# Norm weights applied to the tokens before they are turned, and another order of work in the turn between stages

## What is computed

```python
def rms_norm(x, g):
    y = x * lax.rsqrt(jnp.mean(x * x, axis=-1, keepdims=True) + EPS)
    return y * g

y = stage(rms_norm(x, pre_g[l]))          # ffn, hybrid, memory, ffn / sparse, relu
x = x + scale * rms_norm(y, post_g[l])    # scale 0.5 or 1
```

## Time and profile before

| | |
|---|---|
| runs, us | 1981.7, 1980.12, 1981.13; median 1981.13 |
| profiled execution, us | 1982.36, span 1980.6 |
| PE busy | 1877.0 us (95%) |
| DVE, ACT, POOL busy | 1309.5, 1084.0, 199.5 us |
| mean granted TensorE clock | 0.988 of full |
| DMA | 333 MB, mean 168 GB/s |

### The profile page before, as it was taken

How to read it: one execution, slowest core, us unless ns; L and a number is a source line. 1 busy time by engine, 2 the same in 40 slices (tenths; PEclk the granted TensorE clock), 3 DMA queues, 4 the chain that set the end, 5 groups by cost and what they waited for, 6 DMA issues and landing times.

```text
span 1980.6 us, 28155 instructions
## 1 busy us (share of the span) xinstructions
PE 1877.0 (95%) x10911; PEld 1627.6 (82%) x10911; DVE 1309.5 (66%) x1830; ACT 1084.0 (55%) x1647; POOL 199.5 (10%) x252
## 2 busy tenths in 40 slices
PE   6999998999999999999999899999988999988998
PEld 5888897878888888889887778888867888877887
DVE  5776756665766676666675667666866666766665
ACT  5655544555655565554465566556655445755443
POOL 1010101010000011001020000002100110300111
PEclk9999998999999999999999999999999999999999
DMA  8586643234465557657423527555434564533552
GB/s 264 194 283 191 174 156 105 94 137 153 151 221 191 171 175 238 233 138 221 139 67 122 174 87 223 191 188 168 149 128 158 186 199 155 202 107 128 193 190 85
DMA packets 228389, 333.23 MB, mean 168 GB/s; under 512 B 22230, under 2 KB 178016, under 8 KB 228256
## 3 DMA queue, kind: packets, MB, share of 16 engines
q1 hardware_dynamic: 222112, 307.96, 47.9%
q0 software_dynamic: 6144, 23.49, 3.5%
HBM read 330.38 MB, written 1.05 MB: 167 GB/s over the span
## 4 chain that ended last, share of the span: by engine, by line
PE 85%; DVE 7%; ACT 6%; issue 1%; DMA 1%; POOL 0%; DVEq 0%; SPq 0%; ACTq 0%
PE ps L1635 82%; PE ps L1640 3%; ACT region L691 2%; ACT ahl L691 2%; DVE ahl L1102 2%; DVE xn L1094 1%; DVE wlo L1094 1%; ACT whi L691 1%; DVE xs L1102 1%; DVE region L1094 1%; DMA raw<-ffn_w_gate 1%; DVE mlo L1094 0%; DVE sm L1110 0%; DVE region L1102 0%; ACT mhi L691 0%
## 5 line engine op out<-in xcount | busy, mean ns | idle before, releaser
L1094 DVE TENSOR_TENSOR wlo<-raw,whi 128x1024 fp32r<-128x1024 f32 (+2 forms) x458 | 559.7, 1222 | 199.2 <-ACT whi L691 162.1
L691 ACT ACTIVATE whi<-raw 128x1024 fp32r<-128x1024 f32 (+2 forms) x458 | 483.0, 1055 | 61.6 <-PE ps L1635 15.1
L1635 PE MATMUL ps<-ahl,whi 128*128 128x512 f32 (+1 forms) x1936 | 434.7, 351 | 2.5 <-DVE region L1094 2.1
L1635 PEld LDWEIGHTS ps<-ahl,whi 128*128 128x128 f32 x1936 | 333.4, 190 | 44.9 <-DVE region L1094 2.3
L1635 PE MATMUL ps<-whi,ahl 128*128 128x512 f32 (+2 forms) x1160 | 319.5, 352 | 32.8 <-DVE ahl L1102 28.5
L691 ACT ACTIVATE region<-ps 128x512 f32<-128x512 f32 (+2 forms) x260 | 150.1, 577 | 338.2 <-PE ps L1635 282.4
L1635 PE MATMUL ps<-ahl,wlo 128*128 128x256 f32 x1568 | 271.4, 282 | 0.0
L1635 PEld LDWEIGHTS ps<-whi,ahl 128*128 128x128 f32 x1160 | 207.4, 192 | 68.6 <-DVE ahl L1102 37.9
L1635 PEld LDWEIGHTS ps<-ahl,wlo 128*128 128x128 f32 x1568 | 234.2, 191 | 11.7
L1635 PE MATMUL ps<-wlo,ahl 128*128 128x512 f32 (+2 forms) x580 | 199.2, 343 | 0.0
L1094 DVE TENSOR_TENSOR mlo<-raw,mhi 128x1024 fp32r<-128x1024 f32 x130 | 159.0, 1223 | 54.9 <-ACT mhi L691 44.7
(11 more groups left out here) (164 smaller groups left out, 2417.3 us busy)
## 6 DMA issues: line engine op xcount, KB each, us to landing
raw<-w_ff SPq DMA_DIRECT2D x64, 1024.0 KB, 5.3
raw<-ffn_w_gate SPq DMA_DIRECT2D x44, 1024.0 KB, 5.4
raw<-ffn_w_up SPq DMA_DIRECT2D x44, 1024.0 KB, 5.6
raw<-ffn_w_down SPq DMA_DIRECT2D x44, 1024.0 KB, 4.9
raw<-w_in SPq DMA_DIRECT2D x38, 1024.0 KB, 5.4
raw<-w_out SPq DMA_DIRECT2D x16, 1024.0 KB, 4.9
raw<-xa_wk SPq DMA_DIRECT2D x8, 1024.0 KB, 5.2
raw<-xa_wv SPq DMA_DIRECT2D x8, 1024.0 KB, 5.1
```

The source lines that it names most:

```text
L691: e.activation(o, i, f, **kw).then_inc(*act.did(*names))
L1094: e.tensor_tensor(o, a, b, op).then_inc(*dve.did(*names))
L1635: m = e.matmul(o, l, r, start=start, stop=stop)
```

## The change

The tokens are multiplied by the pre weights before they are turned: `weighted` on DVE writes `X * g` into `XN`, 512 columns at a time, with `g` from the rotating tiles `GV`, and `turn_tokens` turns `XN`. The list of gain rows gets the pre weights of every stage (twelve loads more), and `GC` goes. `gained_halves` is replaced by `halves`, one copy on ACT and one subtraction on DVE of 128x512.

The order changes too. T(0,0) and T(0,1) stand one half product later (`x in (13, 15)`). In the product for m=0, T(1,0) stands behind 11 of 16 parts or 5 of 8, T(1,1) behind 14 or 7. The scales are turned in front of the last part. On ACT the square of y(1,0) stands between the two hi copies of m=0, and the hi of one more weight item is written before the copies of m=1. POOL's waits for `XN` to be free become waits for T(1,1). The last `turn` (s=12) is as before.

```diff
+        name = {"ffn": f + "_pre_g", "hybrid": "mix_pre_g", "memory": "xa_pre_g", "sparse": "g_pre_mix_2",
+                "relu": "g_pre_ffn_2"}[kind]
+        out.append(((s, "pre"), [(0, A[name][l, :])]))
         if kind == "hybrid":
...
-            e.dma_start(GC[:, :], A["g_cols"][:, :]).then_inc(*const_in["gc"].did(("in",)))
...
                     gain_after(s, "post")
+                gain_after(s, "pre")
 
...
-                q.wait_ge(*dve.at("x", s, 1, 1))
+                q.wait_ge(*pe.at("a_turned", s, 1, 1))
...
-            def gained_halves(s, m, half):
...
-            def post_square(s, m):
+            def post_square(s, m, columns=(0, 1)):
-                for n in range(2):
+                for n in columns:
...
-                gained_halves(s, 0, 0)
-                gained_halves(s, 0, 1)
+                halves(s, 0, 0, 0)
                 if s:
-                    post_square(s, 1)
+                    post_square(s, 1, (0,))
+                halves(s, 0, 1, 1)
+                if s:
+                    post_square(s, 1, (1,))
                 row_square(s, 0)
                 split_to(i0 + 1)
-                gained_halves(s, 1, 0)
-                gained_halves(s, 1, 1)
+                if s:
+                    split_to(i1 + 1)
+                halves(s, 1, 0, 2)
+                halves(s, 1, 1, 3)
                 row_square(s, 1)
                 split_to(i1 + 1)
                 if kind_of(s) != "sparse":
...
+                    if s < 12:
+                        weighted(s, m, h)
+
+            def weighted(s, m, h):
+
+                g, c = gain_here(s, "pre"), tokens(m, h)
+                names = [("xn", s, m, h)]
+                if (m, h) == (1, 1):
+                    names.append(("gain", gain_no[s, "pre"]))
+                tt(XN[:, c], X[:, c], g[:, h * 512:h * 512 + 512], ALU.mult, *names)
 
             def post(s, m):
+                if s == 0:
+                    q.wait_ge(*x_in[m].at("x", m))
+                    weighted(s, m, 0)
+                    weighted(s, m, 1)
+                    return
                 post_weigh(s, m, 0)
                 post_var(s, m)
                 post_weigh(s, m, 1)
...
-                if s:
-                    post(s, 0)
-                else:
+                post(s, 0)
+                if s == 0:
                     split_to(0)
-                gained_halves(s, 0, 0)
-                gained_halves(s, 0, 1)
-                if s:
-                    post(s, 1)
+                halves(s, 0, 0, 0)
+                halves(s, 0, 1, 1)
+                post(s, 1)
                 mean_square(s, 0)
                 split_to(i0 + 1)
-                gained_halves(s, 1, 0)
-                gained_halves(s, 1, 1)
+                halves(s, 1, 0, 2)
+                halves(s, 1, 1, 3)
...
-                if s > 11:
-                    return
-                if s:
-                    q.wait_ge(*dve.at("x", s, m, half))
-                else:
-                    q.wait_ge(*x_in[m].at("x", m))
-                for k in range(4):
-                    c = m * DM + (half * 4 + k) * 128
-                    turned(PS[:, 2 * m + half, k * 128:(k + 1) * 128], X[:, c:c + 128], 128, *([("a_turned", s, m, half)] if k == 3 else []))
+                if s < 12:
+                    q.wait_ge(*dve.at("xn", s, m, half))
+                    blocks(s, m, half, 2 * m + half)
 
             def turn(s):
                 it, by_k = first_items(s), BY_K[kind_of(s)]
 
-                def product(m, part):
-                    last, k0 = len(it) - 1, 0
-                    for i, n in enumerate(it):
+                def scales():
+                    for m in range(2):
+                        q.wait_ge(*pool.at("r2", s, m))
+                        turned(PS[:, 7, m * 128:(m + 1) * 128], r2[:, m:m + 1].broadcast_to([128, 128]), 128, *([("r2_turned", s)] if m else []))
+                parts = [(i, n, kk) for i, n in enumerate(it) for kk in range(items[n][2])]
+                def product(m, ahead):
+                    for x, (i, n, kk) in enumerate(parts):
+                        if x in ahead:
+                            ahead[x]()
                         nk, w = items[n][2:4]
                         if w == 584:
                             outs = [(PS[:, m, 0:292], slice(0, 292)), (PS[:, 4 + m, 0:292], slice(292, 584))]
                         else:
                             outs = [(PS[:, m, 0:w] if by_k else PS[:, m, i * 256:(i + 1) * 256], slice(0, w))]
-                        for kk in range(nk):
-                            if part != (0 if i == 0 else 2 if i == last and kk >= nk - max(1, nk // 4) else 1):
-                                continue
-                            hi, lo = weights(n)
-                            k = k0 + kk if by_k else kk
-                            q.wait_ge(*dve.at("a", s, m, k // 4))
-                            ms = slice(m * 128, (m + 1) * 128)
-                            for o, c in outs:
-                                names = []
-                                if kk == nk - 1 and c.stop == w:
-                                    names = [("used", n)] if m else []
-                                    names += [("first", s, m)] if i == last else []
-                                three(o, ahv[:, k, ms], alv[:, k, ms], hi[:, kk, c], lo[:, kk, c], k == 0, k == 7, *names)
-                        k0 += nk
+                        hi, lo = weights(n)
+                        k = x if by_k else kk
+                        q.wait_ge(*dve.at("a", s, m, k // 4))
+                        ms = slice(m * 128, (m + 1) * 128)
+                        for o, c in outs:
+                            names = []
+                            if kk == nk - 1 and c.stop == w:
+                                names = [("used", n)] if m else []
+                                names += [("first", s, m)] if n == it[-1] else []
+                            three(o, ahv[:, k, ms], alv[:, k, ms], hi[:, kk, c], lo[:, kk, c], k == 0, k == 7, *names)
 
                 if s == 0:
                     turn_tokens(0, 0, 0)
                     turn_tokens(0, 0, 1)
-                product(0, 0)
-                turn_tokens(s, 1, 0)
-                product(0, 1)
-                turn_tokens(s, 1, 1)
-                product(0, 2)
-                product(1, 0)
-                product(1, 1)
-                if kind_of(s) != "sparse":
-                    for m in range(2):
-                        q.wait_ge(*pool.at("r2", s, m))
-                        q.wait_ge(*dve.at("a", s, 1, 0))
-                        turned(PS[:, 7, m * 128:(m + 1) * 128], r2[:, m:m + 1].broadcast_to([128, 128]), 128, *([("r2_turned", s)] if m else []))
-                product(1, 2)
+                count = len(parts)
+                product(0, {count * 11 // 16: lambda: turn_tokens(s, 1, 0), count * 7 // 8: lambda: turn_tokens(s, 1, 1)})
+                product(1, {count - 1: scales} if kind_of(s) != "sparse" else {})
 
             def up_tile(hi, lo, f, bank, half, xh, xl, *names):
                 o = PS[:, bank, half * 256:(half + 1) * 256]
...
-                    if x in (12, 14):
+                    if x in (13, 15):
```

More of the change, by code:

```diff
@@ L230, in gain_rows @@
     return out
-def gain_columns(inputs):
-    out = []
-    for kind, l, f in STAGES:
-        name = {"ffn": f + "_pre_g", "hybrid": "mix_pre_g", "memory": "xa_pre_g", "sparse": "g_pre_mix_2",
-                "relu": "g_pre_ffn_2"}[kind]
-        out.append(np.asarray(inputs[name])[l].reshape(8, 128).T)
-    return np.ascontiguousarray(np.concatenate(out, axis=1))
 def home_of(items):
@@ L287, in build @@
         FOLD = sb("fold", 32)
-        GC = sb("gc", 96)
         NM = sb("nm", 48)
@@ L295, in build @@
         x_in = [Done(sem(f"x_in{i}"), 16) for i in range(2)]
-        const_in = {n: Done(sem(n + "_in"), 16) for n in ("ident", "small", "masks", "pe", "ps", "w2", "pos", "gc")}
+        const_in = {n: Done(sem(n + "_in"), 16) for n in ("ident", "small", "masks", "pe", "ps", "w2", "pos")}
         region_in = Done(sem("region_in"), 16)
@@ L717, in halves @@
                 put(columns(ahv, m, half), PS[:, bank, :].rearrange("p (k n) -> p k n", k=4), ACT.Copy, ("a_hi", s, m, half))
-            def gained_halves(s, m, half):
-                bank = 2 * m + half
-                q.wait_ge(*pe.at("a_turned", s, m, half))
-                q.wait_ge(*const_in["gc"].at("in"))
-                for k in range(4):
-                    f = half * 4 + k
-                    put(ahv[:, f, m * 128:(m + 1) * 128], PS[:, bank, k * 128:(k + 1) * 128], ACT.Copy,
-                        *([("a_hi", s, m, half)] if k == 3 else []), scale=GC[:, s * 8 + f:s * 8 + f + 1])
-            def post_square(s, m):
+            def post_square(s, m, columns=(0, 1)):
                 scale = 1.0 / (32.0 * TIMES[s])
-                for n in range(2):
+                for n in columns:
```

(20 more changed lines are left out.)

1 line of the change is left out of this document (removed).

## The result

The changed kernel took 1964.66 us (median of 4 runs, 1962.34 to 1965.32) against 1981.41 us (4 runs): a ratio of 0.9913, interval 0.9895 to 0.993. Beside later experiments it was timed again: 1962.18 us against 1982.07, 0.9905 (0.9891 to 0.9918). So the change wins 17 to 20 us. The forecast was 25.

What follows compares the result with a forecast made beforehand. TensorE was taken as the bound, with its waits at the turns between stages. Gains 19.6+4.0-0.3-0.6+2.3 = 25.0 us gave a forecast of 1956 us, own range 1952 to 1961.

Steps and rivals of the forecast that it cites:

- The turn: Between stages, into ffn, memory and relu: shorter hi and lo win 2.8 us per sixteen-part turn, 19.6 over seven.
- into hybrid: The two turns into hybrid stages, with eight parts: 2.0 us won each, 4.0 together.
- The row of 0.692: Profile row of a similar DVE operation, taken to price each new gain product at 0.69 us, plus 0.03 until the next.
- The start: At the program's start the product begins some 1.1 us earlier and a 1.24 us stop shrinks to nothing: 2.3 us won.
- two 512-column products or 5.8 us of `wq` hide the same delay: Behind ffn and memory turns, the delay from turning the scales later, about 0.3 us, was claimed to be covered.
- 0.3 each there as well: The loss per ffn or memory stage, 0.3 us, if nothing covered the later scales.
- The sparse turns: Into two sparse stages DVE's lo of index weights ends 0.2 us later: no gain, 0.15 lost each, 0.3 together.
- The relu chain: Behind product(1) into two relu stages, the first hidden tile comes about 0.3 us later: minus 0.6 together.
- The gain loads: Twelve more 0.5 MB loads issued by GpSimd behind the roots of each turn; no cost was counted in the sum.
- Given back inside the stages: Rival: weight splits due 2.8 us earlier and thin margins return half of that gain; about 1968 us, chance 0.17.
- More is won: Rival: all stops in sixteen-part turns go, about 3.1 us each, and the start gives 4; about 1951 us, chance 0.10.
- Slower: Rival: the gain loads hold up weight tiles, up to 4.1 us each, 49 us lost; 2005 us, chance 0.03.

Runs made afterwards that it cites:

- Runs 1 to 4: Four follow-ups: new order alone on the kernel before, 1.0023; changed kernel with old order, 0.9924; with T(1,0) behind half the parts, 0.9924; with each gain product twice, 1.006.
- run 1: Kernel before with only the new order on TensorE and ACT, hi and lo still in four pieces: 1987.95 us, ratio 1.0023.
- Run 5: Changed kernel with the scales turned before part 12 of 16 (4 of 8) of product(1) instead of before the last part: 1956.12 us, ratio 0.9862.
- run 2: Changed kernel with the gain product and single hi and lo, but the old order everywhere: 1969.75 us, ratio 0.9924.
- run 8: Changed kernel without eleven of its twelve new gain loads, the product taking the post norm's row (other numbers computed): 1957.67 us, ratio 0.9876.
- run 11: Changed kernel with earlier scales, the sparse index weights' lo ahead of the last renewal, and T(1,0) behind part 8 at the start alone: 1952.65 us, ratio 0.9851.
- run 9: Changed kernel with the product taking the post norm's row, but all twelve gain loads made and not read: 1962.11 us, ratio 0.9904.

## Why the prediction was right, and where its sum was too large

- **The turn.** The product's 0.69, one hi, one lo, the vanished stops: each as worked out. 2.70 us instead of 2.8 in the ffn turn, 2.76 and 2.81 into memory, 1.83 (19.38 to 17.55) instead of 2.0 into hybrid. Runs 1 to 4 show the parts: 0.9 of the product's length is on the path (the worked-out turn holds it as a term), T(1,0)'s new place is worth 1.06, and the order without the short chain costs 0.2 in the turn. The row of 0.692 was the right price: 48 of them took 692 ns in the mean, not the 0.59 of the table in the Trainium skill (VectorE: DVE Perf Modes, the section on the TRN2 errata). The trace bears out the other formula there, which the skill gives for an fp32 addition of two tensors.
- **The start** came out at 2.40 instead of 2.3 by luck. The first product starts 1.8 us earlier (17.23, before 19.02) and not 1.1, in a place that moves by 0.56 between kernels with the same start; from there to the next item it is 1.0 less instead of 1.2, and 0.35 is given back behind it.
- **The mis-sized term: the later scales.** The prediction said that "two 512-column products or 5.8 us of `wq` hide the same delay". Into memory `wq` does: stage 6 came out as forecast. In ffn nothing hides it: 0.35 us behind the turn in each ffn stage, the "0.3 each there as well" that the prediction named for the case without cover. The cover was reckoned for ACT's copy alone; behind the copy stand the gate's tail, four pieces of weights' lo (5.2 us of DVE) and `hlo`, which had been 0.07 us ahead of its use. It is not that TensorE is 2.7 us ahead now: in run 1 it isn't, and the 0.35 is lost all the same. Run 5 gives it back. The other 0.1 of each 0.45 is the turn. In three stages this makes 1.35 us.
- **The sparse turns.** The wait was the right one: DVE's lo ends last, and T(1,0)'s earlier start is hidden. Its size was not: the lo ends 12.4 us behind the first renewal where it ended at 12.0, and T(1,1) comes 0.4 later, not 0.15. Net over both stages it was 1.27 lost, 0.97 beyond the forecast: 0.5 by this, the rest by what lies outside the turn, with a further fall of the clock in one stage and one less in the other.
- **The relu chain.** The 0.3 us of longer stop was right (2.48 for 2.12; the place of the scales is not its only cause, since run 2, with the old place, has 2.13 in one relu stage and 2.48 in the other). What it does to the clock was in no step: 1.7 us in stage 11. Stage 9 had its fall before, too, and so came out as forecast. That the longer stop brought on the fall of stage 11 is likely from the counts below (14 falls behind 17 stops of 2.48, one behind three of 2.12), not shown.
- **The gain loads.** Put at nothing, they cost 4 to 5.5 us by runs 8 and 9, of which 1.1 us is seen: 0.4 in stage 2, which run 8 gives back and earlier scales do not (run 11), 0.5 in GpSimd's last DRAIN, and some hundredths in each ffn stage. How they would bring on more falls was not found, and with one trace each it stays open whether they do; that it isn't the other numbers is shown by run 9.
- **The rivals.** "Given back inside the stages" (1968): a fifth and not half of the gain came back, and not by its mechanism, splits that must be done 2.8 us earlier; what is lost in ffn is lost in run 1 too, with a turn no shorter. Its premise of a dearer product fell. "More is won" (1951) was right that the stops go, T(1,0)'s with them, but the turn won 2.7 and not 3.1. "Slower" fell by a factor of ten in its price.

Forecast minus profile, 25.0-20.0 = 5.0: 1.35 ffn, 0.30 memory, 0.97 sparse, 1.76 relu, 0.53 the rest, 0.17 hybrid, less 0.10 at the start. The hybrid and sparse entries are within what two executions of one kernel differ by. By the medians it is 16.8 in the first measurement and 19.9 in the second; single executions of one kernel lie 1 to 9 us apart.

## What to carry to other kernels

When a signal is moved later in an order (the scales, by one part), follow the work behind it on the other engines to the last thing that uses it, not only to the first covered item, and look up how early that was before: a chain that was ready 0.07 us ahead passes the whole delay on. Cut a stage's time behind the turn, too. The 0.55 us of "the order alone" were 0.2 of one cause and 0.35 of another, and only the cut told them apart. Moving places in an order and shortening a chain are to be tried together; each alone told the wrong thing here. And a stop has two prices, its length and what the clock does behind it, so a stop that grows from 2.1 to 2.5 us, or one that can be split in two, is worth a look of its own.

## What the runs showed of the chip

The stop in front of the first item of a relu stage, over all fourteen traces (the changed kernel has two), against the granted clock behind it; below it, stops of the sparse stages, over the same traces, for the lo of the index weights and, further on, the one stop of 4.2 us that each has:

| stage: stop, us | cases | with a fall to 0.50 during it or within 6 us behind it |
|---|---|---|
| relu: 2.48 | 17 | 14 |
| relu: 2.12 to 2.13 | 3 | 1 |
| relu: 1.50 | 4 | 0 |
| relu: 0.19 to 0.29 | 4 | 0 |
| sparse: 4.24 to 4.25 | 28 | 28 |
| sparse, index weights: 2.85 to 2.87 | 2 | 2 |
| sparse, index weights: 2.12 to 2.15 | 12 | 6 |
| sparse, index weights: 1.32 to 1.41 | 4 | 0 |

Nearly every fall is one of 1.7 us lost (3.4 us at 0.50, which is 1.2 GHz), or two of them end to end, and the ffn stages, where TensorE stands for 1.0 us at most once the start is past, had none before and after the change, nor in any other run (1.2 us at most). The length of the stop does not settle it alone: three of the stops of 2.48 had no fall behind them, half of those of 2.1 in the sparse stages had one, the start of the program, with stops of 5 to 13 us, had none, and in the hybrid stages falls came behind two or three stops of 0.9 to 1.0 in a row (302 us in the changed kernel). One kernel had 1.7 and 5.1 us lost in the same sparse stage in two executions. In relu stage 9 a fall cost 1.4 to 1.6 us (from the first hidden tile to the next renewal 166.8 to 166.9 us with it, 165.4 without, both behind stops of 2.48). What decides then stays open. That the relu stops of 1.5 us and less had none, and that filling the stop removed the fall in both relu stages, is what these runs show.
